# A gated linear attention layer: k turned through memory instead of on TensorE, and the third head's o as well

## The reference, cut to what matters

```
hn = rmsnorm(x, norm_mix_g)
q, k, v, r, a_low = split(hn @ w_in)
log_a = log_sigmoid(a_low @ w_a2 + b_a) / 16
lc = cumsum(log_a)                       # within a chunk of 64
scores = where(past, (q*e^lc)(k*e^-lc)^T, (q*e^-lc)(k*e^lc)^T)
o = scores @ v + (q*e^lc) @ s_prev       # s: state of 128 x 256 for each head
s = g * s + (k*e^(lend-lc))^T @ v        # from chunk to chunk
o = rmsnorm(o) * silu(r);  h = x + o @ w_out
h = h + (silu(hf @ w_g) * (hf @ w_u)) @ w_down,  hf = rmsnorm(h)
```

## Time and profile before

| | |
|---|---|
| time, median of 3 runs (lowest to highest) | 2171.36 us (2170.52 to 2171.55) |
| time of the profiled execution | 2170.81 us |
| its span, first to last instruction | 2169.1 us |
| TensorE busy, share of the span | 2139.3 us, 99% |
| VectorE busy | 1405.3 us, 65% |
| ScalarE busy | 821.5 us, 38% |
| GpSimd busy | 1628.3 us, 75% |
| mean granted clock of TensorE | 0.997 of full |

### The profile page before, as it was taken

One profiled execution on the slowest core, in us unless ns is written; L12 is line 12 of the kernel. 1 busy time (PEld: TensorE's weight loads), 2 busy tenths in 40 slices (PEclk: granted clock), 3 DMA queues, 4 the chain that ended last, 5 costly groups with the idle time before them and its releaser, 6 DMA issues.

```text
span 2169.1 us, 27736 instructions
## 1 busy us (share of the span) xinstructions
PE 2139.3 (99%) x9858; PEld 1772.6 (82%) x9858; DVE 1405.3 (65%) x1808; ACT 821.5 (38%) x1453; POOL 1628.3 (75%) x1294
## 2 busy tenths in 40 slices
PE   8999999999999999999999999999999999999997
PEld 6888888888888888788888888788888888888886
DVE  6455545654565454388887856657666667978796
ACT  4233434343344332344444433444444422142223
POOL 7646675667566756798898878988888887777784
PEclk9999999999999999999999999999999999999999
DMA  5332365346533666655455468434434587758782
GB/s 179 107 88 79 125 205 157 115 126 200 159 117 119 216 187 210 249 180 197 177 189 180 170 218 342 173 136 148 173 126 175 213 322 300 276 227 353 276 315 115
DMA packets 246665, 413.14 MB, mean 190 GB/s; under 512 B 34208, under 2 KB 177568, under 8 KB 237568
## 3 DMA queue, kind: packets, MB, share of 16 engines
q1 hardware_dynamic: 211568, 368.83, 48.5%
q10 hardware_dynamic: 34960, 42.54, 5.8%
HBM read 278.14 MB, written 133.17 MB: 190 GB/s over the span
## 4 chain that ended last, share of the span: by engine, by line
PE 64%; DVE 2%; DMA 1%; POOL 1%; SPq 1%; ACT 1%; issue 1%; ACTq 0%; DVEq 0%; POOLq 0%
PE ps L1064 12%; PE ps L1065 12%; PE ps L1069 12%; PE ps L1138 6%; PE ps L1139 6%; PE ps L1143 6%; PE ps L797 1%; PE ps L798 1%; PE ps L801 1%; PE ps L771 1%; DMA hop<-stage 1%; PE ps L773 1%; PE ps L772 1%; PE ps L784 1%; PE ps L783 1%; PE ps L787 1%
## 5 line engine op out<-in xcount | busy, mean ns | idle before, releaser
L703 POOL TENSOR_TENSOR w_op<-w_raw,w_op 128x512 fp32r<-128x512 f32 x330 | 480.5, 1468 | 105.7 <-ACT w_op L1160 102.9
L1064 PE MATMUL ps<-x_op,w_op 128*128 128x512 f32 x1232 | 480.5, 390 | 2.9 <-DVE u L1881 2.5
L1065 PE MATMUL ps<-x_op,w_op 128*128 128x512 f32 x1232 | 480.1, 390 | 0.0
L691 POOL TENSOR_SCALAR ring_hi<-raw 128x512 fp32r<-128x512 f32 x256 | 175.8, 687 | 278.1 <-issue 141.1
L694 POOL TENSOR_TENSOR ring_lo<-raw,ring_hi 128x512 fp32r<-128x512 f32 x256 | 352.1, 1376 | 21.3
L1160 ACT ACTIVATE w_op<-w_raw 128x512 fp32r<-128x512 f32 x330 | 202.8, 627 | 375.9 <-POOL w_raw L721 154.3
L1069 PE MATMUL ps<-x_op,w_op 128*128 128x512 f32 x1232 | 329.9, 390 | 0.0
L1064 PEld LDWEIGHTS ps<-x_op,w_op 128*128 128x128 f32 x1232 | 231.5, 188 | 52.3 <-issue 4.3
L1069 PEld LDWEIGHTS ps<-x_op,w_op 128*128 128x128 f32 x1232 | 231.7, 188 | 48.3 <-POOL w_op L703 0.2
L1065 PEld LDWEIGHTS ps<-x_op,w_op 128*128 128x128 f32 x1232 | 231.5, 188 | 47.9
L1138 PE MATMUL ps<-w_op,hid 128*128 128x512 f32 x616 | 240.7, 391 | 1.5 <-issue 0.7
(11 more groups left out here) (221 smaller groups left out, 4075.2 us busy)
## 6 DMA issues: line engine op xcount, KB each, us to landing
hop<-stage SPq DMA_DIRECT2D x154, 512.0 KB, 2.9
hid<-hop SPq DMA_DIRECT2D x70, 1024.0 KB, 9.3
raw<-in_gla_w_in SPq DMA_DIRECT2D x192, 256.0 KB, 3.3
w_raw<-in_ffn_w_gu SPq DMA_DIRECT2D x176, 256.0 KB, 4.0
w_raw<-in_ffn_w_down SPq DMA_DIRECT2D x88, 256.0 KB, 4.5
xop<-x_stage ACTq DMA_DIRECT2D x42, 512.0 KB, 4.2
x_op<-xop SPq DMA_DIRECT2D x36, 512.0 KB, 8.9
raw<-in_gla_w_out SPq DMA_DIRECT2D x64, 256.0 KB, 3.2
```

The source lines that it names most:

```text
L691: pool.tensor_scalar(ring_hi[:, u, :], raw[:, p, u % 2, :], 1.0, 0.0, ALU.mult, ALU.add).then_inc(unit_hi, 1)
L703: pool.tensor_tensor(shaped(q, tile[:, 1, :]), source(q, i), shaped(q, tile[:, 0, :]).bitcast(F32), ALU.subtract).then_inc(op_ready[i], 1)
L1064: pe.matmul(out, w_hi, x_op[i][:, m, 0, :], start=m == 0 and i < 3, stop=False, skip_group_check=i > 2)
L1065: pe.matmul(out, w_hi, x_op[i][:, m, 1, :], start=False, stop=False, skip_group_check=i > 2)
```

## The change

k no longer goes through TensorE. ScalarE's queue stores `kf` in memory in four pieces (`k_kept`), laid out so that the 32x32 blocks are exchanged, then waits until they have landed and loads it back (`k_back`); VectorE transposes the blocks within (`kt`), and `k_hi` and `k_lo` are made from that. In heads 0 to 2 this turn comes behind `under_vr`, in the fourth head ahead of it. TensorE's transposes of k and its wait for `k_tok_done` ahead of the next q go. The third head's o goes through memory as the first two, but by ScalarE's queue: stored behind the third head, loaded behind the fourth head's stores of k, transposed and split in the fourth head. In the fourth head ScalarE's root of the next x stands behind the silu, VectorE's root and its first three scalings behind the state's steps, and TensorE's first `turn_next` behind the second unit of `w_out` instead of the first.

```diff
 def make_scores(n):                                   # TensorE
     pe.wait_ge(k_scaled, 2 * (n + 1))
-    for t in range(NT):
-        tok = slice(t * P, (t + 1) * P)
-        ins = pe.transpose(ps[:, 0, tok], kf[:, tok], ident[:, :])
-    ins.then_inc(kt_done, 1)
-    if n % H == 1 or n % H == 2:
+    if n % H > 0:
         pe.wait_ge(og_done, NT * n)
...
-                    pe.wait_ge(k_tok_done, n + 1)
                     column_units(i + 3, 0, ps[:, 0, :])
...
-                    if hd == 2:
-                        turn_o(n)
...
-                    if more and m == 0:
+                    if more and m == 1:
                         turn_next(b, 0)
 def head(b, hd, under_vr, under_o):                   # ScalarE
-    act.wait_ge(kt_done, n + 1)
-    split_hi(k_hi[:, :], ps[:, 0, :]).then_inc(k_hi_done, 1)
+    act.wait_ge(k_scaled, 2 * n + 1)
+    for j in range(4):
+        act.dma_start(k_kept[:, :].rearrange("(i s) (t j r) -> j s t i r", i=4, t=4, j=4)[j],
+                      kf[32 * j:32 * j + 32, :].rearrange("s (t i r) -> s t i r", t=4, i=4))\
+            .then_inc(k_moved, 16)
+    if hd == H - 1:
+        load_og(b)
...
     act.activation(scores[CHUNK:, :, CHUNK:], past[CHUNK:, :, CHUNK:], ACT.Copy).then_inc(past_copied, 1)
+    act.wait_ge(k_moved, 16 * (5 * n + 4))
+    if n > 0:
+        act.wait_ge(ds_done, NT * n)
+    act.dma_start(k_back[:, :], k_kept[:, :]).then_inc(k_moved, 16)
     act.wait_ge(scores_ready, 2 * (n + 1))
     split_hi(scores_hi[:, :, :], scores[:, :, :]).then_inc(scores_hi_done, 1)
-    under_vr()
+    if hd < H - 1:
+        under_vr()
+    turned_k_hi(n)
+    if hd == H - 1:
+        block_turned_hi(b, H - 2)
+        under_vr()
...
+def store_og(b):
+    act.wait_ge(og_done, NT * (b * H + H - 1))
+    act.dma_start(og_kept[:, :].rearrange("(t p) c -> p t c", p=P), og[:, :, :]).then_inc(og_moved, 16)
+def load_og(b):
+    act.wait_ge(og_moved, 16 * (5 * (3 * b + H - 2) + 1))
+    by_32 = og_kept[:, :].rearrange("(m s) (i c) -> i s m c", s=32, i=4)
+    for i in range(4):
+        act.dma_start(og_by_32[32 * i:32 * i + 32, :, :], by_32[i]).then_inc(og_moved, 16)
...
-                turned_o_hi(b, H - 2)
+                store_og(b)
                 if b < NB - 1:
-                    head(b, H - 1, lambda: square_next(b), lambda: None)
+                    head(b, H - 1, lambda: square_next(b), lambda: root(ROOTS[b, "ahead"], slice(NT, 2 * NT)))
 def head(b, hd, under_vr, under_o):                   # VectorE
-    dve.wait_ge(k_hi_done, n + 1)
-    dve.nop(nofuse=True)
-    split_lo(k_lo[:, :], ps[:, 0, :], k_hi[:, :]).then_inc(k_tok_done, 1)
...
-    under_vr()
+    if hd < H - 1:
+        under_vr()
+    dve.wait_ge(k_moved, 16 * 5 * (n + 1))
+    dve.transpose(kt[:, :], k_back[:, :]).then_inc(k_turned, 1)
+    if hd == H - 1:
+        turn_o_blocks(b, H - 2)
+    dve.wait_ge(k_hi_done, n + 1)
+    split_lo(k_lo[:, :], kt[:, :], k_hi[:, :]).then_inc(k_tok_done, 1)
+    if hd == H - 1:
+        block_turned_lo(b, H - 2)
+        under_vr()
...
-                def next_under_vr():
+                def next_under_o():
                     norm_next(b)
                     scale_next(b, 0)
-                def next_under_o():
                     scale_next(b, 1)
                     scale_next(b, 2)
...
-                turned_o_lo(b, H - 2)
```

More of the change, by code:

```diff
@@ L104, in gla_layer @@
         qf, qb, kf, kb = (qk_scaled[:, n, :] for n in range(4))
+        k_at = MIX + 4 * (2 * KD * T + H * T + 4 * T + 2 * T)
+        k_back, kt = (sb(n, k_at + 4 * T * m, [P, T]) for m, n in enumerate(("k_back", "kt")))
         softlog = qk_scaled
@@ L168, in gla_layer @@
         hres = nc.dram_tensor("hres", [SEQ, D], F32)
+        k_kept = nc.dram_tensor("k_kept", [P, T], F32)
         og_kept = nc.dram_tensor("og_kept", [T, DV], F32)
@@ L197, in gla_layer @@
             sem(n) for n in ("k_scaled", "vr_done", "v_hi_done", "v_done", "r_silu", "r_done"))
-        kt_done, k_hi_done, k_tok_done, past_done, future_done, past_copied, scores_ready, scores_hi_done, scores_split \
-            = (sem(n) for n in ("kt_done", "k_hi_done", "k_tok_done", "past_done", "future_done", "past_copied",
+        k_turned, k_hi_done, k_tok_done, past_done, future_done, past_copied, scores_ready, scores_hi_done, scores_split \
+            = (sem(n) for n in ("k_turned", "k_hi_done", "k_tok_done", "past_done", "future_done", "past_copied",
                                 "scores_ready", "scores_hi_done", "scores_split"))
@@ L203, in gla_layer @@
                              "oT_lo_done"))
-        og_stored, og_loaded, oT_blocks = sem("og_stored"), sem("og_loaded"), sem("oT_blocks")
+        og_moved, oT_blocks = sem("og_moved"), sem("oT_blocks")
+        k_moved = sem("k_moved")
         wo_done, wo_added = sem("wo_done"), sem("wo_added")
@@ L724, in _ @@
                 if q == 0:
-                    pool.wait_ge(oT_done, 4 * NB)
+                    pool.wait_ge(oT_done, 2 * NB)
                 ahead = 3 if q == SECOND_HALF + 1 else 0
@@ L882, in make_scores @@
                 pe.wait_ge(k_scaled, 2 * (n + 1))
-                for t in range(NT):
-                    tok = slice(t * P, (t + 1) * P)
-                    ins = pe.transpose(ps[:, 0, tok], kf[:, tok], ident[:, :])
-                ins.then_inc(kt_done, 1)
-                if n % H == 1 or n % H == 2:
+                if n % H > 0:
                     pe.wait_ge(og_done, NT * n)
                 elif n > 0:
-                    pe.wait_ge(oT_lo_done, 6 * (n // H) + (4 if n % H else 0))
+                    pe.wait_ge(oT_lo_done, (H + 1) * (n // H))
                 if n > 0 and n % H == 0:
@@ L1007, in _ @@
                 pe.wait_ge(r_silu, n + 1)
-                pe.wait_ge(oT_lo_done, 6 * b + 4)
+                pe.wait_ge(oT_lo_done, (H + 1) * b + 3)
                 more = b < NB - 1
@@ L1014, in _ @@
                     if m == 6:
-                        pe.wait_ge(oT_lo_done, 6 * (b + 1))
+                        pe.wait_ge(oT_lo_done, (H + 1) * (b + 1))
                     if m == KV and more:
@@ L1303, in block_turned_hi @@
             def block_turned_hi(b, hd):
-                act.wait_ge(oT_blocks, 2 * b + hd + 1)
+                act.wait_ge(oT_blocks, 3 * b + hd + 1)
                 parts = slice(2 * hd, 2 * hd + 2)
@@ L1309, in turned_o_hi, with turned_k_hi @@
                 for j in range(2):
-                    act.wait_ge(oT_done, 4 * b + 2 * (hd - 2) + j + 1)
+                    act.wait_ge(oT_done, 2 * b + j + 1)
                     act.nop(nofuse=True)
                     split_hi(oT_hi[:, 2 * hd + j, :], ps[:, 6 + j, :]).then_inc(oT_hi_done, 1)
+            def store_og(b):
[6 more added lines that the diff above has]
+                    act.dma_start(og_by_32[32 * i:32 * i + 32, :, :], by_32[i]).then_inc(og_moved, 16)
+            def turned_k_hi(n):
+                act.wait_ge(k_turned, n + 1)
+                split_hi(k_hi[:, :], kt[:, :]).then_inc(k_hi_done, 1)
             def square_next(b):
@@ L1317, in square_next @@
                     square(SQUARES[b, "ahead"], t, xs[:, t, :], NT)
-                root(ROOTS[b, "ahead"], slice(NT, 2 * NT))
             act.dma_start(g_mix[:, :], norm_mix_g.to_broadcast([P, D])).then_inc(mix_loaded, 16)
@@ L1949, in _ @@
                     scale_qk(b * H + hd + 1)
-                turned_o_lo(b, H - 2)
                 more = b < NB - 1
-                head(b, H - 1, next_under_vr if more else (lambda: None), next_under_o if more else (lambda: None))
+                head(b, H - 1, lambda: None, next_under_o if more else (lambda: None))
                 if more:
```

12 lines of the change are left out of this document (6 added, 6 removed).

## The result

The changed kernel took 2220.67 us (median of 4 runs, 2218.55 to 2226.63), the kernel before 2170.94 us on the same chip (4 runs, 2169.03 to 2171.55): ratio 1.0239, 95% interval 1.0226 to 1.0253. It is slower, as forecast, but by 49.7 us and not by 8.

A forecast was written before the change was run, and what follows sets the result against it. TensorE, with work for 99% of the span, was taken to bound the kernel. -9.2 + 7.5 (fourth heads) + 4.8 (clock) + 5.0 (heads 1 and 2) = +8.1 us, so 2179 us was predicted, range 2168 to 2188.

The forecast's parts named there:

- What leaves TensorE: Transposes of k in 13 of 16 heads (5.7 us) and of the third head's o in four blocks (3.4): -9.2 us.
- The fourth heads: Blocks 0 to 2: `v_lo` comes late behind k's round trip and the squares; TensorE waits 2.5 us each, +7.5 us.
- 3.2 us as the 256 KB of w_out, and 0.2 us for the 512 KB ahead of it in the queue: Fourth heads: landing of k's load back, issued 5.1 us after `kf` and landed at 8.5.
- four issues at about 0.4 us: Fourth heads: ScalarE issues k's four stores, the last at 1.25 us after `kf`; landing of 3.7 puts them at 4.95.
- The estimate that the prediction takes from the Trainium skill: Fixed 2.0 us plus bytes over 436 GB/s: store 2.2 us, load back 2.6, sum 1.8 smaller; set aside for the rows.
- Heads 1 and 2: Blocks 1 to 3: k's turn adds 2.2 us before silu; waits 1.65, 2.2 and 1.2 in three heads, +5.0 us.
- the load back ahead of the operand stores in ScalarE's queue: Heads 1 and 2, blocks 1 to 3: costs about what TensorE's earlier start gives, so left out.
- The next x: Root and scalings moved behind the state's steps; `xT_lo` nearly on time: nothing, at most 1 us a block at risk.
- The clock: TensorE's clock falls to half behind the late fourth heads of three blocks, 1.6 us each: +4.8 us, bounds 0 and 5.1.
- An idle time of 2.5 us is beyond both: Fourth heads: the wait exceeds earlier idle times of 1.85 us (clock fell) and 1.42 (held), so a fall is expected.
- the 128-byte stores are slow: Rival: k's stores take twice 3.7 us, delaying fourth and at least five other heads; +24 us, 2203; chance 0.06.
- the 5 us that the prediction gave as a sign of being wrong: Sign: the prediction is wrong if a store of k lands in over 5 us.

The follow-up runs named there:

- e_k_alone: The changed kernel with the third head's o on TensorE as before, only k through memory: 2197.47 us, 1.0134 of the kernel before.
- e_wide_pieces: The changed kernel with k's four stores writing whole 2 KB rows instead of 128-byte pieces, so k's transpose comes out wrong: 2209.32 us, 1.0175.
- e_scalings_alone: The kernel before with only the next x's root and scalings moved later and its first turn one unit later: 2174.51 us, 1.0023.
- e_all_moved: The changed kernel reordered: k's turn between operands, two scalings first, squares ahead of `k_hi`, load back before o's loads, o's turn later: 2201.58 us, 1.0145.
- e_traffic_free: The kernel before plus k's stores and load back with no reader, those of the fourth heads issued where ScalarE idles: 2176.80 us (9 runs), 1.0033.
- e_x_late_too: The changed kernel with k on TensorE as before, block 1's x loaded in block 0's fourth head: 2190.09 us, 1.0093 of the kernel before.
- e_x_collides: k on TensorE, o through memory, block 1's x load in block 0's fourth head held until the third head's decays are made: 2195.27 us, 1.0118.
- e_traffic_only: The kernel before plus k's stores behind `scores_hi` and load back behind silu, with no reader and TensorE's transposes in use: 2190.85 us, 1.0098.
- e_o_late: The kernel before with the third head's o through memory, every step in an idle place, the loaded tile in its own memory: 2171.20 us, 1.0005.

## Why the prediction was off, step by step

The step that failed is the price of the transfers. From the end of `kf` to the landing of k's load back the prediction counted 8.5 us. It took 11.4, 12.4 and 15.2 us in blocks 0, 1 and 2, and the mid heads, where the prediction let ScalarE's wait for its own stores go at nothing, lost 16.0 where it had 5.0.

**What leaves TensorE** (-9.2): right. 96 matmuls are gone, and the waits for `xf` are 0.78 where 0.34 + 0.44 was forecast.

**The fourth heads** (+7.5, measured +18.6 in blocks 0 to 2, with another 3.66 in the fourth, costed at nothing). The mechanism was right: the squares stand behind the round trip, and `v_lo` is late. So were the ends of the sum: in block 0 `kf` ends at 162.48, the load back is issued 5.1 us later, as forecast, and TensorE comes at 177.66, 15.2 behind where 15.3 was forecast. What failed in block 0 is the landing "3.2 us as the 256 KB of w_out, and 0.2 us for the 512 KB ahead of it in the queue". It took 6.3 (167.60 to 173.87), beside o's four loads, which had only just been issued; in e_k_alone it took 2.4. That is the whole of block 0's difference, 5.20 against 2.5, and in block 3 the same landing took 7.1.

In blocks 1 and 2 the load back landed in 3.0 and 4.0 us, but it went out 9.4 and 11.3 us behind `kf` in place of 5.1. It has to wait for k's stores. Their landing, forecast at 3.7 us, took 5.9 to 7.9, and the last landed at 403.10 and 634.50, 0.02 and 0.03 us ahead of the load back (403.12 and 634.53). ScalarE's other road came to the same place, since o's store, "4.2 us to land", took 8.1 and 8.2 and held the loads of o until 400.10 and 629.67. The "four issues at about 0.4 us" took 4.2 and 5.1 us, so that the last store was issued 3.5 and 3.6 us behind `kf` in place of 1.25. The landings were late together: the next x, o's store and k's stores were in flight at once. With 2 KB pieces (e_wide_pieces) k's stores still took 5.9 to 6.5 us there, without o's store (e_k_alone) 3.7 to 5.4. ScalarE in block 2:
```profile
621.50 0.37 ACTq L1333 DMA_DIRECT2D og_kept<-og  x1
623.29 5.13 ACTq L1270 DMA_DIRECT2D k_kept<-qk_scaled  x4
629.67 3.59 ACTq L1339 DMA_DIRECT2D og_by<-og_kept  x4
...
634.53 0.35 ACTq L1284 DMA_DIRECT2D k_back<-k_kept  x1
```
The earlier trace rows gave medians over the span, and I read them as the price at a place where, in blocks 1 and 2, the next x's 2 MB are always under way. The estimate that the prediction takes from the Trainium skill, "DMA: Bandwidth & Descriptors", on the anatomy of one DMA, rests on a fit that the page gives for transfers issued by GpSimd. These are issued by ScalarE and SP, and k's stores took 4.0 us in the median where that estimate has 2.2.

**Heads 1 and 2** (+5.0, measured 13.2, and 16.0 with two heads 0). The three heads that the sum names have 10.9. The 2.2 us of added operations were right for head 1 of block 3 (1.86). I left out "the load back ahead of the operand stores in ScalarE's queue" as worth nothing; there the error is. ScalarE waited 30.8 us in 11 places for k's stores ahead of `scores_hi`, so the operand stores behind it go out late and their tiles come free late. e_wide_pieces bears this out: ScalarE waited 14.5 us there, and silu's waits were 9.2. In head 2 of block 3 that wait is 4.46 us, and the next operand split waits 6.05 for a store; TensorE then 6.58. Head 0 of block 0, head 0 of block 1 and head 2 of block 1, costed at nothing, gave 0.59, 2.20 and 2.27.

**The next x** (0, measured 5.6). I had `xT_lo` "within half a microsecond of when it is wanted". Three scalings take 5.06 us (191.68), then `og`, the fourth scaling and `xT_lo` follow, while TensorE has 1.86 us less work than that. e_scalings_alone shows it without anything else: +5.1 us. The price could have been had from the trace of before: in block 1 `xT_lo` of the first tile ended at 414.27 there and its transposes began at 416.36, so the room was 2.1 us; moved in ahead of it are the root's pieces, 1.2 us, and the third scaling, 5.06 - 2.48 = 2.6. That makes 1.7. Half of those 2.6 us is GpSimd's doing: the three scalings took 1.29, 1.63 and 2.30 us, the last two begun while GpSimd was at a split of the weights.

**The clock** (+4.8, about 13). Falls came where forecast, behind each late fourth head, but also behind waits of 2.20, 2.47, 3.66 and 6.58 us (not behind 2.27), seven in all where three were forecast. Read from the trace's record of the clock, those behind 2.20 and 2.47 last 3.4 us and the other five 6.8. In block 0 4.0 us of one lay under work and cost 2.0; the seven cost 14.3. The prediction's step from "An idle time of 2.5 us is beyond both" to a fall came true, but the length of an idle time alone doesn't decide it. In e_all_moved TensorE idled 2.67 us ahead of the same instructions in blocks 0 and 1, and the clock was 1.00 from 195.8 to 202.0 and 0.72 from 422.8 to 429.0. The earlier trace rows has a fall behind 1.85 us, and the changed kernel none behind 2.36 us at 1407.6.

**The rivals.** That the 128-byte stores are slow, at 0.06, was the nearest. A store of k landed in up to 7.9 us, past the 5 us that the prediction gave as a sign of being wrong, and e_wide_pieces gave 11.4 us back. It had 2203, and the time came out above it too, because the pieces were only a fourth of the loss.

The sum with measured terms: -9.2 + 22.3 (four fourth heads) + 16.0 + 5.6 + 13 = +47.7, which is what the span grew by. That it fits to a tenth proves little: the 13 is itself what the busy times leave over, and 0.8 us of waits that the kernel before had and a few small new ones for the weights, both left out, nearly cancel. Every term after the first was too small. The two kinds of heads were so for one reason: landings and issues were taken at medians, and all that stands behind them is one chain. The clock's term followed the waits. The next x's has its own cause, VectorE's work.

What stays open: how the 7 us of e_traffic_free divide, since its runs lie 11 us apart and the profiled one is the lowest; whether the small pieces cost by size or by number; and why o's four loads and the load back took up to 6.4 us in block 0 and only 4.0 in block 1.

## What to carry to other kernels

Price a transfer by the rows of the place and the moment where it will stand, with what the other queues have in flight then, not by its median over the kernel; and count the issue, since four small-piece stores held ScalarE for 2.6 to 5.1 us. A round trip through memory may replace 0.44 us of work only where its consumer is many microseconds away, and a wait for one's own store stands ahead of all that its queue does next. Before taking work from the busiest engine, ask what it covered: here even the best order for o gave back 3.1 of 3.4 us as waits on engines that had been just in time.

## What the runs showed of the hardware

- The issue of a DMA isn't a constant: k's stores took 0.58 us at least, 0.65 in the median and 2.06 at most, and four together 2.6 us in block 0 but 5.1 in block 2, with the next x in flight.
- Two queues don't shield each other: a 512 KB store on ScalarE's queue landed in 3.2 us with no load of x in flight (e_x_late_too) and in 9.1 when SP's queue had started 2 MB 1.1 us earlier (e_x_collides).
- The same scaling of 128x1024 on VectorE took 1.28 us in one place and 2.2 in another (e_traffic_only, e_o_late), with nothing changed in it. Of the 204 scalings of the next x in all 17 traces, the 62 that began while GpSimd was at a `ring_lo` took 1.38 to 2.31 us, and the 89 that began with GpSimd at no split took 1.27 to 1.29. Where a scaling began first and `ring_lo` met it, as at 411.94 in the kernel before, `ring_lo` took 2.29 us (median 1.29).
- In five of the changed kernel's seven falls TensorE's clock fell while the engine still idled, so that part of the stretch at 1.2 GHz cost nothing; in block 0 2.8 of 6.8 us. Behind the waits of 2.20 and 2.47 us it fell 0.9 and 0.4 us after work had begun again, and all 3.4 us counted.
